# Writing the relative bias rows to memory once and replicating them from memory to memory

## The reference

```python
mod = silu(c) @ w_ada + b_ada                   # six vectors of 1024 for each of 9 sequences
h   = rmsnorm(x) * (1 + scale1) + shift1
q, k, v, cb, cc, cv, ga, gb = split(h @ w_in)   # one projection, 512 columns each for q, k and v
s   = q @ k.T * HEAD_DIM**-0.5                  # 8 heads; a band of 9 chunks of 64 keys
rel = clip(q_pos - k_pos, -128, 128) + 128
s   = s + rel_bias[:, rel]                      # learned bias, 257 values for each head
p   = softmax(s);  o = p @ v
```

## Time and profile before

| | |
|---|---|
| median of the runs | 1897.24 us |
| the profiled execution | 1901.71 us, of which the span from first to last instruction is 1899.9 us |
| mean granted TensorE clock | 0.94 |
| PE, PEld, DVE, ACT, POOL busy | 88%, 73%, 52%, 40%, 11% of the span |
| chain that ended last | PE 83%, DVE 7%, DMA 3%, "another core or an unknown queue" 2%, ACT 2% |

### The profile page before, as it was taken

The page is one execution under the profiler, slowest core; times in us unless marked ns, Lnnn a source line. Parts: engine busy times, 40 slices in busy tenths (PEclk is TensorE's granted clock), DMA queues, the critical chain, the costliest instruction groups (busy, mean ns, idle before and its releaser), DMA issues.

```text
span 1899.9 us, 22477 instructions
## 1 busy us (share of the span) xinstructions
PE 1674.5 (88%) x8467; PEld 1395.4 (73%) x8467; DVE 981.8 (52%) x1156; ACT 764.2 (40%) x869; POOL 218.1 (11%) x336
## 2 busy tenths in 40 slices
PE   7984999999989989999999897189999999999920
PEld 1244987887549989999998786168888888888820
DVE  0451011554321263222213555848998988989947
ACT  0221122664111112111112222147877877877734
POOL 2003501110000000000000000401000000000035
PEclk9996999999999999999999998589999999999965
DMA  9757622002412111121114434089999999999863
GB/s 343 273 100 195 211 75 72 1 1 91 158 68 70 42 36 37 51 79 53 48 50 137 168 116 150 12 312 405 420 421 414 413 416 416 412 413 415 357 228 137
DMA packets 137403, 371.34 MB, mean 195 GB/s; under 512 B 10699, under 2 KB 69107, under 8 KB 112626
## 3 DMA queue, kind: packets, MB, share of 16 engines
q1 hardware_dynamic: 113440, 289.92, 40.1%
q0 software_dynamic: 18976, 62.93, 10.2%
q10 hardware_dynamic: 4914, 17.49, 2.3%
HBM read 324.49 MB, written 47.89 MB: 196 GB/s over the span
## 4 chain that ended last, share of the span: by engine, by line
PE 83%; DVE 7%; DMA 3%; issue 2%; another core or an unknown queue 2%; ACT 2%; POOL 0%; SPq 0%; POOLq 0%; DVEq 0%; ACTq 0%; PEldq 0%
PE ps L1579 21%; PE ps L1581 21%; PE ps L1580 21%; PE ps L1562 4%; PE ps L1706 3%; PE ps L1687 2%; PE ps L1769 2%; PE ps L1746 2%; PE ps L1893 1%; PE ps L1696 1%; DMA bada<-in_b_ada_dram 1%; PE ps L1843 1%; PE ps L1688 1%; DMA mraw<-in_w_e_down_dram 1%
## 5 line engine op out<-in xcount | busy, mean ns | idle before, releaser
L1094 DVE TENSOR_TENSOR mlo<-mraw,mhi 128x2048 fp32r<-128x2048 f32 x188 | 420.8, 2283 | 14.9 <-ACT mhi L948 13.8
L948 ACT CAST mhi<-mraw 128x2048 fp32r<-128x2048 f32 x192 | 357.9, 1913 | 30.2 <-DMA mraw<-in_w_e_down_dram 29.1
L1579 PE MATMUL ps<-hTh,ring_r 128*128 128x384 f32 x864 | 293.3, 339 | 38.8 <-DVE ring_r L1094 30.8
L1581 PE MATMUL ps<-hTh,ring_r 128*128 128x384 f32 x864 | 292.0, 338 | 0.0
L1580 PE MATMUL ps<-hTl,ring_r 128*128 128x384 f32 x864 | 291.9, 338 | 0.0
L1579 PE MATMUL ps<-mhi,xTh 128*128 128x512 f32 x512 | 204.6, 400 | 4.0 <-DVE xTl L1094 2.4
L1581 PE MATMUL ps<-mhi,xTl 128*128 128x512 f32 x512 | 201.6, 394 | 0.0
L1580 PE MATMUL ps<-mlo,xTh 128*128 128x512 f32 x512 | 201.6, 394 | 0.0
L1579 PEld LDWEIGHTS ps<-hTh,ring_r 128*128 128x128 f32 x864 | 165.0, 191 | 40.4 <-DVE ring_r L1094 29.0
L1094 DVE TENSOR_TENSOR ring_r<-ring_f,ring_r 128x1024 fp32r<-128x1024 f32 x56 | 68.3, 1224 | 203.0 <-ACT ring_r L758 202.7
L1580 PEld LDWEIGHTS ps<-hTl,ring_r 128*128 128x128 f32 x864 | 165.1, 191 | 0.0
(11 more groups left out here) (302 smaller groups left out, 2578.4 us busy)
## 6 DMA issues: line engine op xcount, KB each, us to landing
mraw<-in_w_e_gate_dram SPq DMA_DIRECT2D x64, 1024.0 KB
mraw<-in_w_e_up_dram SPq DMA_DIRECT2D x64, 1024.0 KB
mraw<-in_w_e_down_dram SPq DMA_DIRECT2D x64, 1024.0 KB, 7.3
aring<-in_w_ada_dram SPq DMA_DIRECT2D x24, 1024.0 KB
ring_f<-in_w_in_dram SPq DMA_DIRECT2D x80, 256.0 KB, 4.5
y_d<-yy ACTq DMA_DIRECT2D x32, 512.0 KB, 7.7
y_d<-zrow POOLq DMA_DIRECT2D x68, 128.0 KB, 3.9
kc<-in_cache_attn_k_dram SPq DMA_DIRECT2D x8, 1024.0 KB, 5.2
```

The costliest lines, as they stand in the source:

```text
L948: nc.scalar.copy(mhi[j][:], mraw[j][:]).then_inc(s["gu_hi" if j < 4 else "d_hi"], 1)
L1094: V.tensor_tensor(out, value, high.bitcast(F32), ALU.subtract).then_inc(sig, 1)
L1579: mm(out, xh, wh, start=start, stop=False)
L1581: return mm(out, xl, wh, start=False, stop=stop)
```

## The change

A new array in memory, `relone_d`, holds the 8 rows once. POOL writes it from `relrow`, waits for that, and then fills `relrow_d` with one DMA from memory to memory; the outer dimension of that DMA is the replica (128), the inner one the head. POOL then waits for both. On ScalarE the waits for `rel_out` and `mod_out` move from ahead of the evacuation of q to ahead of the evacuation of v. ScalarE's wait for `rel_out` keeps the value 16, which is now reached when the 8 rows have left SBUF.

```diff
         modrep_d = dram("modrep_d", (NS_TOK, 4 * D))
+        relone_d = dram("relone_d", (H, P - 1 + BAND))
         relrow_d = dram("relrow_d", (H, P, P - 1 + BAND))
...
             pool.wait_ge(s["rel_sb"], 2)
-            pool.dma_start(relrow_d, relrow[:].unsqueeze(1).to_broadcast([H, P, P - 1 + BAND])
+            pool.dma_start(relone_d, relrow[:]).then_inc(s["rel_out"], 16)
+            pool.wait_ge(s["rel_out"], 16)
+            pool.dma_start(relrow_d.rearrange("h p c -> p h c"), relone_d.unsqueeze(0).to_broadcast([P, H, P - 1 + BAND])
                            ).then_inc(s["rel_out"], 16)
-            pool.wait_ge(s["rel_out"], 16)
+            pool.wait_ge(s["rel_out"], 32)
             pool.wait_ge(s["n1_h"], NT)
...
             weights_high_to(2)
-            act.wait_ge(s["rel_out"], 16)
-
-            for r in range(3):
-                act.wait_ge(s[f"mod_out{r}"], MOD_OUT[r])
             g = 0
...
                 nc.scalar.copy(kk[:, i % 2, :], ps[:, 4 + g % 4, :]).then_inc(s["gev_kout"], 1)
                 g += 1
+            act.wait_ge(s["rel_out"], 16)
+            for r in range(3):
+                act.wait_ge(s[f"mod_out{r}"], MOD_OUT[r])
             for t in range(NT):
```

## The result

| | before | after |
|---|---|---|
| median | 1897.41 us (4 runs, 1896.85 to 1898.03) | 1867.76 us (4 runs, 1864.79 to 1870.14) |
| ratio, with its 95% interval | | 0.9843 (0.9826 to 0.9860) |
| the profiled execution | 1901.71 us | 1864.79 us |

The kernel is 29.65 us faster by the medians (26.6 to 33.0 by the interval); 31.76 were predicted. Timed again twice, beside the kernel before on another chip each time, it gave 1868.3 against 1897.12 and 1866.33 against 1898.49: 28.8 and 32.2 us.

A forecast was written before the change was run, and what follows sets the result against it. TensorE's chain was held by a 33.53 us piece, waiting for unit 1's weights, delayed by the bias rows' slow DMA. 28.85 + 2.91 = 31.76 us off the median 1897.24 gives 1865.5 us, range 1861 to 1871 (0.84).

The forecast's parts named there:

- The hole: TensorE idles 28.68 us between units 0 and 1; unit 1's weights land late with the bias rows, ScalarE's waits not decisive.
- 28.85 us from the hole: With unit 1's weights ready, its first product on TensorE moves from 170.86 to 142.01 us: 28.85 us gained.
- the slow restart: TensorE runs at half clock after the idling, from 170 to 177 us; without the idling 2.91 us more are gained.
- the other slow start: TensorE's slow start at 136.26 us, after 2.36 us of idling, was expected to stay.
- From the one execution to the median: Profiled execution 1901.71 to 1869.95 us; it is 4.47 us above the median, so the sum off 1897.24 gives 1865.5.
- The copy's cost: POOL's memory-to-memory copy of the rows: 8.2 us on 16 engines at 24 GB/s, issued at 107, complete by about 119.
- The landing of the 8 rows: POOL's 24.5 KB write, issued at 101.90 us, was put at landing at 107, with bounds of 104 and 109.
- The rivals: Slow copy or later traffic keeps part of the gain (0.08); hole stays, 1897 (0.03); copy below 44 GB/s or otherwise slower (0.05).
- a slow copy: Copy takes 63 us again, unit 2 late: 1888 (within 0.08); or at 25 GB/s: 1951 (within 0.05).

The follow-up runs named there:

- the runs with extra rows: Changed kernel plus a write of 96 or 64 extra replicas from SBUF to an unread scratch array, ahead of the copy: 1889.41 us and 1876.99 us.

## Why the prediction was right, and where its terms were off

The forecast was 1865.5 us with a range of 1861 to 1871; 1867.76 was measured.

*The hole belongs to unit 1's weights, not to ScalarE's waits.* Right, and shown from both sides: the waits alone give nothing, the copy alone gives everything.

*28.85 us from the hole.* Right: the first product of unit 1 follows the last of unit 0 by 0.17 us.

*2.91 us from the slow restart.* Right: the clock is 1.00 from 134 to 170 us. Between the first product after the norm stage (136.26 before, 134.56 after) and TensorE's last product of v (314.14 and 279.21 in the two timelines) the stretch shrinks from 177.88 to 144.65 us, by 33.23. The sum of 31.76 leaves 1.47, and that is the other slow start, which I had expected to stay: before, unit 0's third chunk began at half clock (0.69 us for its first product), after it did not (0.44). In both later traces of the changed kernel it did again; this is one of them:

```profile
135.44 0.69 PE L1581 MATMUL ps<-hTh,ring_r 128*128 128x384 f32 x1 [2.36 <-DVE hTl L1109]
```

In these two the same stretch takes 146.17 us (135.00 to 281.17) and 146.05 (135.44 to 281.49), 31.71 and 31.83 less than before: the sum to within 0.1 us. So this piece comes and goes between executions of one kernel, and in the result's trace it fell on the fast side by luck.

*From the one execution to the median.* The two profiled executions differ by 36.92 us, the medians by 29.65, and neither is the sum. Of the 36.92, 33.23 lie in the stretch above, 1.70 ahead of everything the change touches (the norm's first transposes start at 72.45 and 70.75 us) and 2.0 behind v. The profiled execution before lies at the upper end of its kernel's runs (1901.71, where 19 later runs lie between 1894.53 and 1901.79), the one after is the lowest of the first four (1864.79 to 1870.14). The terms hold; an execution carries up to some 5 us of its own, so the 2.3 us between forecast and median can't be put down to a term.

*The copy's cost.* The step that was mis-sized, in a term that the sum doesn't contain. I had 8.2 us of moving, at 24 GB/s on each of 16 engines, and 12 us from issue to landing (107 to 119). The copy moved at 250 GB/s, 15.6 on each engine, which is 12.6 us for 3.14 MB, and landed 15.5 us after its issue, just outside the 10 to 15 that I had named. The rate of one busy engine could not be multiplied by 16: eight engines reached 23 each, sixteen 15.6, and padded rows brought the sixteen to 303 GB/s, 19 each. What held them to 15.6 stays open. The landing of the 8 rows was expected 5.1 us after their issue and took 3.7. Neither matters, since unit 1 had landed by 106.7 and ScalarE was free for it only at 133.15.

*The rivals.* No run of a copy out of memory came near a slow copy. Their common premise, that a copy which holds the engines delays the weights, is what the runs with extra rows show; the reckoning that a unit lands when the slow rows end is too kind, since what is queued behind them counts as well. The changed kernel has a small case of it: unit 2, issued at 110.80, landed at 121.0, just behind the copy (119.6), at no cost, because its cast came after 133.

## What to carry to other kernels

When an engine waits for a load that is usually quick, look at what the other queues hold on the DMA engines in that stretch: here a share near one half with few bytes moving was a slow DMA that occupied eight of them, and a load spread over all 16 was as late as its last part on those eight. Rows that leave a few partitions many times can be written once and replicated from memory: 50 GB/s became 250. Before a wait is moved, read which of two neighbouring waits ended last; here the one that looked guilty cost nothing.

## What the runs showed of the hardware that I had not expected

- A queue's issue can stall behind another queue's slow DMA: SP's two issues of unit 2 took 32.34 us beside the old write and 0.93 us without it.
- Two queues on a busy engine got through packet for packet, not byte for byte: 80 packets of each in 10 us of the kernel before, 0.49 MB of rows and 0.04 MB of weights.
- The copy with the replica outside uses 16 engines at 15.6 GB/s each, with the head outside 8 engines at 23: 250 against 181 GB/s, not twice as much. Rows padded to 3072 bytes bring the first to 303.
- Executions of one kernel differ by up to 8 us (1894.92 to 1902.71 for the kernel before on one chip), and which short waits are followed by half clock differs between them; a gain of 2 us can't be read from two profiles.
